# Two blocks on one core: down products that end output by output, an adaptive row by dot products, one norm statistic in place of two roots, and a lead of two half blocks

## The chip, the cores and the metric

The kernel runs on one core of a Trainium2 chip. A core has five engines with a queue of their own each: TensorE (matrix products, page name PE, its weight loads PEld), VectorE (DVE), ScalarE (ACT), GpSimd (POOL) and SyncE (SP), which here issues DMAs. The engines meet only through semaphores. The metric is the device time of one execution in microseconds (us); lower is better.

## The reference

Two layers on a sequence of 512 tokens of width 1024. Each begins with an adaptive vector, from which shifts, scales and gates come. What the change touches is the feed-forward part of the first layer, the norm that closes it and the norm that opens the second layer:

```python
x = x + g2 * conv_glu(modulate(rms_norm(x, norm2_w), sh2, sc2), ffn_w_up, ffn_conv_w, ffn_conv_b, ffn_w_down)
return rms_norm(x, final_norm_w)              # end of the first layer
...
mod = (silu(c_2) @ ada_w_2 + ada_b_2)         # 6 x 1024 values for the second layer
sh1, sc1, g1, sh2, sc2, g2 = jnp.split(mod, 6, axis=-1)
h = rmsnorm(x, mix_norm_pre) * (1.0 + sc1) + sh1
x = x + g1 * rmsnorm(windowed_gqa_sink(h, w_qkv, ...), mix_norm_post)
h = rmsnorm(x, ffn_norm_pre) * (1.0 + sc2) + sh2
x = x + g2 * rmsnorm(swiglu(h, w_in, w_out), ffn_norm_post)
```

The hidden width is 2816, the weights are float32, and so is the result.

## The kernel before

Values lie transposed: channels on the 128 partitions, the 512 tokens along the row, so that a vector of 1024 channels is 8 chunks and the hidden layer 22.

**Products.** Weights come in 92 blocks of 1 MB (128 x 2048). A block in `w_raw` is copied to `w_hi` in a rounded format by ScalarE (`high`, L230), and POOL takes the rest, `w_lo = w_raw - w_hi`, in four instructions (`low`, L239). Activations are split likewise into `h_hi` and `h_lo`. A product is then three matrix products over a chunk, hi·hi, hi·lo and lo·hi (`chunk_products`, L246). Raw, hi and lo have two buffers each, used in turn: `high` and `low` of block b wait until block b-2 is used (`half_used`, counted twice a block), and SyncE loads block b when the split of block b-2 is done (`lo_done`).

**Stages.** Blocks 0 to 11 are the first projection (with context products, L1089, beside it), 12 to 15 the first output projection, 16 to 37 the first up product, 38 to 48 the first down product (L285), 49 to 54 the projection of the second layer, 55 to 58 its output projection, 59 to 80 and 81 to 91 the second up and down product. In the ordinary form a block gives two outputs of 128 channels over all 8 chunks, into banks 0 to 3 in turn. A stage that follows a norm opens with `lead`: as its input chunks come one by one (`h_low`), block b is done chunk by chunk for both outputs, then block b+1 output by output. In the down products a block holds two of the 22 hidden chunks for all 8 outputs; eight banks gather over 11 blocks, and the last block ends them 6 products apart. The hidden pair of each block goes through slots 0 to 3 of `h_hi` (ScalarE, L1375) and `h_lo` (VectorE, L1624).

**Norm.** ScalarE squares each output (L319), VectorE adds the squares (L332), TensorE makes the mean (`mean`, L338), ScalarE its root (L343), VectorE the reciprocal (L347), TensorE spreads it over a bank (`spread`, L354), VectorE scales (L376), ScalarE applies gain and shift in two versions (L363, L366), and VectorE subtracts them (L379). Between the layers two norms follow each other. They are folded: squares with and without the final weight (L1404) are summed apart, and four small steps give a common scale (`fold`).

**The second adaptive vector.** Its weights come as 24 tiles through a ring of two (`ada_ring`, L214). VectorE adds each tile in eight steps of 256 columns to `acc2` (`add_ada2`, L1459 and L1461), one tile after the tap sums of each gated tile of the first up product, and two after it. After the down product TensorE sums `acc2` over the partitions, 48 columns (L1227), and VectorE makes the gains (L1666 to L1671).

The order of the work is written by hand, one program for each engine; every queue is in order. SyncE's loads alternate: a weight block, an adaptive tile.

## Time and profile before

| | us |
|---|---|
| runs shown | 1529.8, 1535.93, 1533.78 (median 1533.78) |
| the profiled execution | 1530.2, of which span 1528.4 |
| busy: PE / DVE / ACT / POOL | 1406.1 / 651.7 / 555.5 / 634.2 |
| granted TensorE clock, mean share | 0.948 |

The durations further on come from the profiled execution. PE is busy for 92% of its span; a busy PE is not PE at its peak, since matrix products are pipelined and their ends are modelled. An instruction for TensorE on float32 data stands as two records in the trace, on the rounded format as one.

### The profile page before, as it was taken

To read this page: it belongs to the slowest core of one execution; us is meant where nothing else is said; L and a number is where in the kernel's file an instruction comes from. 1 tells how busy PE (TensorE), PEld (TensorE's weight loads), DVE (VectorE), ACT (ScalarE), POOL (GpSimd) and SP (SyncE) were. 2 spreads that over 40 slices of the span, in tenths; PEclk is the share of its full clock that TensorE was granted. 3 is DMA by queue.
4 is the path that set the end of the run, shared out by engine and by line. 5 is a ranking of instruction groups with operands and counts; after the bars stand their busy time and mean duration, and the time that the engine had idled before them with its cause. 6 is when DMAs were issued, how large, how long until landed. Compare 5 with 4: busy or idle time off the path is not lost.

```text
span 1528.4 us, 17743 instructions
## 1 busy us (share of the span) xinstructions
PE 1406.1 (92%) x6432; PEld 1130.5 (74%) x6432; DVE 651.7 (43%) x1173; ACT 555.5 (36%) x807; POOL 634.2 (41%) x516
## 2 busy tenths in 40 slices
PE   8699997898678899999899989999979999999995
PEld 1588866686677678888688888655768888888884
DVE  1563478576842665554711163476232000001115
ACT  2512423473322544344222262477235232323221
POOL 0233254124634254545445554433242444444642
PEclk9799998899989899999999979999969999999997
DMA  9124552600012145545422232200111232222221
GB/s 396 55 99 173 194 193 105 166 1 1 1 56 110 64 185 219 206 178 194 192 83 108 82 138 83 83 2 1 52 59 55 85 107 84 108 86 107 83 82 55
DMA packets 26979, 165.45 MB, mean 108 GB/s; under 512 B 2688, under 2 KB 4992, under 8 KB 8496
## 3 DMA queue, kind: packets, MB, share of 16 engines
q1 hardware_dynamic: 24912, 150.10, 26.7%
q10 hardware_dynamic: 2016, 14.68, 2.7%
q8 instruction: 31, 0.51, 0.1%
q14 instruction: 20, 0.16, 0.0%
HBM read 162.64 MB, written 6.32 MB: 111 GB/s over the span
## 4 chain that ended last, share of the span: by engine, by line
PE 82%; DVE 7%; POOL 4%; issue 3%; ACT 2%; DMA 1%; POOLq 0%; SPq 0%; DVEq 0%; ACTq 0%
PE bank L246 46%; PE bank L285 16%; PE bank L1089 3%; PE bank L583 2%; PE bank L563 2%; PE bank L1067 2%; PE bank L444 2%; POOL arena L761 1%; PE bank L1227 1%; POOL arena L763 1%; PE bank L1149 1%; PE bank L573 1%; PE bank L423 1%; PE bank L424 1%; PE bank L354 1%
## 5 line engine op out<-in xcount | busy, mean ns | idle before, releaser
L239 POOL TENSOR_TENSOR w_lo<-w_raw,w_hi 128x512 fp32r<-128x512 f32 x368 | 499.2, 1387 | 693.0 <-ACT w_hi L230 683.1
L246 PE MATMUL bank<-h_hi,w_hi 128*128 128x512 f32 x1120 | 443.9, 396 | 22.6 <-POOL w_lo L239 8.7
L246 PE MATMUL bank<-h_lo,w_hi 128*128 128x512 f32 x1120 | 439.5, 392 | 0.0
L246 PE MATMUL bank<-h_hi,w_lo 128*128 128x512 f32 x1120 | 439.4, 392 | 0.0
L230 ACT ACTIVATE w_hi<-w_raw 128x2048 fp32r<-128x2048 f32 x92 | 176.2, 1915 | 439.4 <-PE bank L285 172.1
L246 PEld LDWEIGHTS bank<-h_hi,w_hi 128*128 128x128 f32 x1120 | 212.8, 190 | 71.9 <-issue 17.2
L246 PEld LDWEIGHTS bank<-h_hi,w_lo 128*128 128x128 f32 x1120 | 212.3, 190 | 44.8
L246 PEld LDWEIGHTS bank<-h_lo,w_hi 128*128 128x128 f32 x1120 | 212.6, 190 | 43.3
L285 PE MATMUL bank<-h_hi,w_hi 128*128 128x512 f32 x352 | 138.0, 392 | 7.2 <-DVE arena L1635 6.3
L285 PE MATMUL bank<-h_lo,w_hi 128*128 128x512 f32 x352 | 137.7, 391 | 0.0
L285 PE MATMUL bank<-h_hi,w_lo 128*128 128x512 f32 x352 | 137.5, 391 | 0.0
L1624 DVE TENSOR_TENSOR h_lo<-arena,h_hi 128x1024 fp32r<-128x1024 f32 x22 | 31.5, 1438 | 183.1 <-ACT h_hi L1375 172.3
L1731 DVE TENSOR_TENSOR arena<-arena,bank 128x512 f32 (+1 forms) x22 | 15.2, 689 | 208.7 <-PE bank L246 208.7
L1461 DVE SCALAR_TENSOR_TENSOR arena<-ada_ring,small,arena 128x256 f32 (+1 forms) x168 | 92.4, 550 | 6.0
L285 PEld LDWEIGHTS bank<-h_hi,w_hi 128*128 128x128 f32 x352 | 66.5, 189 | 22.0 <-DVE arena L1635 6.7
L319 ACT ACTIVATE arena<-arena 128x512 f32<-128x512 f32 (+1 forms) x56 | 33.3, 598 | 122.9 <-DVE arena L1614 37.7
L285 PEld LDWEIGHTS bank<-h_hi,w_lo 128*128 128x128 f32 x352 | 66.5, 189 | 14.0
L285 PEld LDWEIGHTS bank<-h_lo,w_hi 128*128 128x128 f32 x352 | 66.5, 189 | 13.6
L1470 DVE SCALAR_TENSOR_TENSOR arena<-bank,params,arena 128x511 f32<-128x511 f32 (+1 forms) x36 | 25.4, 704 | 119.6 <-ACT arena L1352 87.0
L719 POOL TENSOR_SCALAR arena<-arena,small 128x256 f32<-128x256 f32 (+1 forms) x64 | 32.8, 531 | 55.4 <-DVE small L677 55.4
L539 POOL TENSOR_SCALAR arena<-arena,small 128x512 f32<-128x512 f32 x32 | 21.7, 692 | 73.3 <-DVE small L518 73.3
L1089 PE MATMUL bank<-arena,w_raw 128*128 128x256 f32 x224 | 50.5, 379 | 0.0
(222 smaller groups left out, 1661.5 us busy)
## 6 DMA issues: line engine op xcount, KB each, us to landing
w_raw<-w_dram SPq DMA_DIRECT2D x92, 1024.0 KB, 4.8
ada_ring<-ada_dram SPq DMA_DIRECT2D x30, 1024.0 KB, 4.8
ada_ring<-ada_dram ACTq DMA_DIRECT2D x14, 1024.0 KB, 4.7
arena<-ada_dram SPq DMA_DIRECT2D x4, 1024.0 KB, 9.4
arena<-x_dram SPq DMA_DIRECT2D x2, 2048.0 KB, 11.5
bias_copies<-bias_rows SPq DMA_DIRECT2D x1, 4096.0 KB, 26.3
arena<-bias_copies SPq DMA_DIRECT2D x1, 3072.0 KB, 11.3
out_dram<-arena SPq DMA_DIRECT2D x8, 256.0 KB, 2.1
```

The costliest lines, as they stand in the source:

```text
L230: nc.scalar.activation(w_hi[b % 2][:], w_raw[b % 2][:], ACT.Copy).then_inc(hi_done, 1)
L239: last = nc.gpsimd.tensor_tensor(w_lo[b % 2][:, part], w_raw[b % 2][:, part], w_hi[b % 2][:, part], ALU.subtract)
L246: last = nc.tensor.matmul(bank[:, :], w[:, ft, k, :], x[:, k, :], start=k == 0 and m == 0, stop=k == DC - 1 and m == 2)
L285: last = nc.tensor.matmul(ps[f][:, :], w[:, k, f, :], x[:, 2 * gslot + k, :], start=first and k == 0 and m == 0, stop=last_block and k == ...
L319: nc.scalar.activation(buf[:, k % 2, 0:n], src, ACT.Square).then_inc(sq_done, 1)
L444: last = nc.tensor.matmul(ps[7][:, 0:256], v, pt1[G % 2][:, kb, :], start=kb == 0, stop=kb == 3)
L563: nc.tensor.matmul(ps[u % 3][:, 0:128 * (hi - lo)], q2[:, 2 * g + hq // 2, t * 128:(t + 1) * 128], k2[:, g, hq % 2, lo * 128:hi * 128], st ...
L583: last = nc.tensor.matmul(ps[7][:, :], vtok2[:, lo + kb, g, :], pt2[:, G % 2, kb, :], start=kb == 0, stop=kb == hi - lo - 1)
L719: nc.gpsimd.tensor_scalar(prob2[:, u % 8, 0:w], prob2[:, u % 8, 0:w], row_inv[:, u % 16:u % 16 + 1], 1.0, ALU.mult, ALU.mult).then_inc(s[" ...
L1089: last = nc.tensor.matmul(ps[4 + n % 2][:, 0:CTX], raw[:, n % 2, k, :], HC[:, k, :], start=k == 0, stop=k == DC - 1)
L1461: ins = nc.vector.scalar_tensor_tensor(out=dst, in0=src, scalar=silu_c2[:, k:k + 1], in1=dst, op0=ALU.mult, op1=ALU.add)
L1624: nc.vector.tensor_tensor(h_lo[:, part, :], HID[:, bass.ds(2 * t + 2 * off, 2), :], h_hi[:, part, :], ALU.subtract).then_inc(g_split, 1)
```

## The change

- **Down products.** The hidden weights are laid out anew: 7 blocks by chunk pair as before (chunks 0 to 13), then 4 blocks in the ordinary form (chunks 14 to 21, all eight slots of `h_hi`). So the outputs end one after the other, 24 products apart, and the updates and squares of the first seven run under the products. The very first products go to banks 4 to 7; only those for banks 0 to 3 wait for the last gated tile.
- **The statistic.** The mean is made in two parts: `mean_head` over the sum of seven squares, in the stream before the last chunks, and `mean_last` directly from the eighth square. VectorE adds seven, not eight.
- **The folded norm.** The root for the next input is taken from one statistic: the squares of ScalarE are scaled by `sqrt(final^2 + eps)`, the epsilon is `eps^2`. The scale for the residual is a root of its own, taken after the third affine chunk, and its spread stands inside `lead`.
- **The adaptive vector.** Its weights are transposed, and each tile gives two groups of 128 values by two dot products with a row (`tensor_tensor_reduce`). The row `row2` is spread over all partitions by eight products in the first output projection and copied from two banks by ScalarE. Tiles 20 and 21 are moved behind the first two hidden splits of the down product, 22 and 23 behind its loop; both last loads stand behind both first down blocks.
- **The lead.** Now chunks 0 to 3 of block b, chunks 0 to 3 of block b+1, chunks 4 to 7 of b, then of b+1. This holds for all four leads.
- A dummy root (`sqrt_table`) stands ahead of the squares, so that the table is loaded there.

```diff
-        def lead(pe, b, h_from, ctx_product=None):
+        def lead(pe, b, h_from, ctx_product=None, between=None):
             pe.wait_ge(lo_done, b + 1)
-            for k in range(DC):
+            for k in range(4):
+                pe.wait_ge(h_low, h_from + k + 1)
+                for ft in (0, 1):
+                    chunk_products(b, ft, ps[ft], k)
+            if between:
+                between()
+            pe.wait_ge(lo_done, b + 2)
+            for k in range(4):
+                for ft in (0, 1):
+                    chunk_products(b + 1, ft, ps[2 + ft], k)
+            for k in range(4, DC):
                 if k == DC - 1 and ctx_product:
                     ctx_product(0)
                     ctx_product(1)
...
                     last = chunk_products(b, ft, ps[ft], k)
                     if k == DC - 1:
                         last.then_inc(half_used, 1)
-            pe.wait_ge(lo_done, b + 2)
             for ft in (0, 1):
                 if ctx_product:
                     ctx_product(2 + ft)
-                for k in range(DC):
+                for k in range(4, DC):
                     last = chunk_products(b + 1, ft, ps[2 + ft], k)
                 last.then_inc(half_used, 1)
...
+                return
+            for k in range(2):
+                for f in range(4, DC):
+                    product(k, f)
+            pe.wait_ge(tile_free, bank_free)
+            for k in range(2):
+                for f in range(4):
+                    last = product(k, f)
+                last.then_inc(half_used, 1)
...
+        def mean_head(pe, r, buf, bank):
+            pe.wait_ge(sq_used, 8 * r + 7)
+            for t in range(4):
+                nc.tensor.matmul(ps[bank][:, t:t + 1], buf[:, 2, t * P:(t + 1) * P], con_("mean")[:, 0:1], start=t == 0, stop=False)
+        def mean_last(pe, r, buf, bank):
+            pe.wait_ge(sq_done, 8 * r + 8)
+            for t in range(4):
+                last = nc.tensor.matmul(ps[bank][:, t:t + 1], buf[:, 1, t * P:(t + 1) * P], con_("mean")[:, 0:1], start=False, stop=t == 3)
+                if t == 2:
+                    last.then_inc(sq_used, 1)
+            last.then_inc(mean_done, 1)
...
                 load_block(sp, B_DOWN + u)
+            for u in range(2):
                 load_ada(sp, T["ada2"][22 + u], 46 + u)
             with sp.Fori(0, 5) as i:
                 for u in range(2):
                     load_block(sp, B_DOWN + 2 + u, 2 * i)
             load_block(sp, 50)
             sp.wait_ge(mod2_ready, 1)
+            sp.wait_ge(g_split, 11)
...
+                    down_products(pe, b0 + t, 0, t, bank_free if t == 0 else None)
...
                     for t in (2, 3):
-                        pe.wait_ge(g_split, g0 + t + 1 + 2 * i)
-                        down_products(pe, b0 + t, 2 * i, t % 2, False, False)
...
+                down_products(pe, b0 + 6, 0, 0)
+                pe.wait_ge(lo_done, b0 + 8)
+                for k in (4, 5, 6, 7, 2, 3, 0, 1):
+                    if k in (2, 0):
+                        pe.wait_ge(g_split, g0 + (10 if k == 2 else 11))
+                    for ft in (0, 1):
+                        last = chunk_products(b0 + 7, ft, ps[ft], k, None, 1)
+                        if k == 1:
+                            last.then_inc(half_used, 1)
+                for f in range(2, DC):
+                    b = b0 + 7 + f // 2
+                    if f % 2 == 0:
+                        pe.wait_ge(lo_done, b + 1)
+                    for k in range(DC):
+                        last = chunk_products(b, f % 2, ps[f], k, None, DC - 1)
+                        if f == DC - 1 and k == 5:
+                            mean_head(pe, r, SQ2, 4)
+                    last.then_inc(half_used, 1)
+                mean_last(pe, r, SQ2, 4)
...
+            for k in range(DC):
+                last = nc.tensor.matmul(ps[5 + k // 4][:, k % 4 * P:(k % 4 + 1) * P], silu_c2[:, k:k + 1].to_broadcast([P, P]), ident,
+                                        start=True, stop=True)
+            last.then_inc(row2_done, 1)
...
-            pe.wait_ge(down_free, 1)
-            pe.wait_ge(ada_used, 48)
-            for f in range(48):
-                last = nc.tensor.matmul(ps[0][:, f:f + 1], acc2[:, f * 128:(f + 1) * 128], ones[:, 0:1], start=True, stop=True)
-            last.then_inc(col_done, 1)
...
+            down(B_DOWN, 0, 3, F_QKV)
+            spread(pe, 3, 5).then_inc(scale_out, 1)
...
+                last = nc.tensor.matmul(ps[4][:, 4 + t:5 + t], SQF[:, 2, t * P:(t + 1) * P], con_("mean")[:, 0:1], start=True, stop=True)
+            last.then_inc(res_mean, 1)
+            def residual_spread():
+                pe.wait_ge(res_scale, 1)
+                spread(pe, 3, 6, of=res_col).then_inc(scale_out, 1)
+            lead(pe, B_QKV, 16, between=residual_spread)
...
+            nc.scalar.activation(final_eps, par_("final"), ACT.Square).then_inc(root_final, 1)
+            act.wait_ge(root_final, 1)
+            nc.scalar.activation(final_eps, final_eps, ACT.Sqrt, bias=con_("eps")).then_inc(root_final, 1)
...
+                act.wait_ge(half_used, 2 * b0)
+                hidden_high(slice(18, 20), 4)
+                hidden_high(slice(20, 22), 6)
                 high(act, b0 + 2)
...
+                        act.wait_ge(half_used, 2 * b0 + 2 * (t - 1) + 4 * i)
+                        hidden_high(bass.ds(2 * t + 4 * i, 2), 2 * (t % 2))
                         high(act, b0 + t + 1, 2 * i)
...
+                sqrt_table()
+                high(act, b0 + 8)
+                high(act, b0 + 9)
+                for f in range(3):
+                    squares_of(f)
+                high(act, b0 + 10)
+                squares_of(3)
+                squares_of(4)
+                if blocks_after:
+                    high(act, b0 + 11)
+                for f in range(5, DC):
+                    squares_of(f)
+            sqrt_table()
+            for k in range(2):
+                act.wait_ge(row2_done, 1)
+                nc.scalar.activation(row2[:, 512 * k:512 * k + 512], ps[5 + k][:, :], ACT.Copy).then_inc(row2_out, 1)
...
+            def both_squares(f):
                 act.wait_ge(down_free, f + 1)
-                squares(act, 3, f, XR[:, f, :], SQ2)
+                squares(act, 3, f, XR[:, f, :], SQ2, scale=final_eps[:, f:f + 1])
...
-                nc.scalar.activation(SQF[:, f % 2, :], XR[:, f, :], ACT.Square, scale=par_("final")[:, f:f + 1]).then_inc(sqf_done, 1)
...
+                nc.scalar.activation(SQF[:, f % 2, :], XR[:, f, :], ACT.Square).then_inc(sqf_done, 1)
...
+            down_act(B_DOWN, F_QKV, both_squares, True)
+            root(act, 3, 4, eps="epseps")
+            high(act, B_QKV + 1)
...
+            def residual_root():
+                act.wait_ge(res_mean, 1)
+                nc.scalar.activation(res_col, ps[4][:, 4:8], ACT.Sqrt, bias=con_("eps")).then_inc(res_root, 1)
+            affine(act, 2, lambda c: gain3[:, c:c + 1], lambda c: mod2[:, c:c + 1], XN2, HB2, residual_root)
...
-                dst = acc2[:, bass.ds(256 * j + 256 * off, 256)]
-                for k in range(8):
...
-                    ins = nc.vector.scalar_tensor_tensor(out=dst, in0=src, scalar=silu_c2[:, k:k + 1], in1=dst,
-                                                         op0=ALU.mult, op1=ALU.add)
...
+                for f in range(2):
+                    src = ada[:, s * BLK + f * D:s * BLK + (f + 1) * D]
+                    last = nc.vector.tensor_tensor_reduce(out=src, in0=src, in1=row2, scale=1.0, scalar=0.0, op0=ALU.mult,
+                                                          op1=ALU.add, accum_out=dots[:, 2 * s + f:2 * s + f + 1])
+                last.then_inc(ada_used, 1)
+                dve.wait_ge(ada_used, 24 + j + 1 + off)
+                two = bass.ds(2 * j + 2 * off, 2)
+                nc.vector.tensor_tensor(mod2[:, two], dots[:, 2 * s:2 * s + 2], par_("adab2")[:, two], ALU.add).then_inc(mod2_part, 1)
...
-                add_ada2(u, 2 * i)
+                if u < 2:
+                    add_ada2(u, 2 * i)
...
+                hidden_low(g0 + 3, slice(18, 20), 4)
+                hidden_low(g0 + 4, slice(20, 22), 6)
+                if with_ada:
+                    add_ada2(20)
+                    add_ada2(21)
...
                 if with_ada:
                     add_ada2(22)
                     add_ada2(23)
...
+                    dve.wait_ge(mod2_part, 24)
...
+                hidden_low(g0 + 9, slice(12, 14), 0)
+                hidden_low(g0 + 10, slice(16, 18), 2)
+                hidden_low(g0 + 11, slice(14, 16), 0)
...
+                dve.wait_ge(half_used, 2 * (B_DOWN + 7) + f + 1)
...
+            normalise(dve, 2, XR, XN2, HB2, 5, residual_scale)
```

The queue of SyncE around the first two down blocks. `ada_ring<-ada_dram` is a load of an adaptive tile, `w_raw<-w_dram` one of a weight block. Before:

```order
L214 ISA
L214 DMA ada_ring<-ada_dram 128x2048
L990 REGISTER_ALU
L990 COMPARE_AND_BRANCH
L223 DMA w_raw<-w_dram 128x2048
L214 DMA ada_ring<-ada_dram 128x2048
L223 DMA w_raw<-w_dram 128x2048
L214 DMA ada_ring<-ada_dram 128x2048
L997 UNCONDITIONAL_BRANCH
L997 ISA
L223 ISA
L223 DMA w_raw<-w_dram 128x2048
```

And now:

```order
L214 ISA
L214 DMA ada_ring<-ada_dram 128x2048
L1018 REGISTER_ALU
L1018 COMPARE_AND_BRANCH
L223 DMA w_raw<-w_dram 128x2048 x2
L214 DMA ada_ring<-ada_dram 128x2048 x2
L1026 UNCONDITIONAL_BRANCH
L1026 ISA
L223 ISA
L223 DMA w_raw<-w_dram 128x2048
L223 ISA
L223 DMA w_raw<-w_dram 128x2048
```

Two weight loads (blocks 38 and 39) stand together, and two adaptive loads behind them, ahead of the loop that begins with block 40.

TensorE at the end of the first down product: L285 is a down product, L1227 the column sums, L1232 and L338 the two statistics, L354 the spreads, L246 the projection. Before:

```order
L285 MATMUL bank<-h_hi,w_lo 128x512
L285 MATMUL bank<-h_hi,w_hi 128x512
L285 MATMUL bank<-h_lo,w_hi 128x512
L285 MATMUL bank<-h_hi,w_lo 128x512
L1227 MATMUL bank<-constants,arena 128x1 x48
L1232 MATMUL bank<-constants,ada_ring 128x1 x4
L338 MATMUL bank<-constants,arena 128x1 x4
L354 MATMUL bank<-constants,small 128x128 x8
L246 MATMUL bank<-h_hi,w_hi 128x512
```

And now (L350 is `mean_head`, L356 `mean_last`, L378 the spread, L1294 the other statistic):

```order
L246 MATMUL bank<-h_lo,w_hi 128x512
L246 MATMUL bank<-h_hi,w_lo 128x512
L350 MATMUL bank<-constants,arena 128x1 x4
L246 MATMUL bank<-h_hi,w_hi 128x512
L246 MATMUL bank<-h_lo,w_hi 128x512
L246 MATMUL bank<-h_hi,w_lo 128x512
L246 MATMUL bank<-h_hi,w_hi 128x512
L246 MATMUL bank<-h_lo,w_hi 128x512
L246 MATMUL bank<-h_hi,w_lo 128x512
L356 MATMUL bank<-constants,arena 128x1 x4
L378 MATMUL bank<-constants,small 128x128 x4
L1294 MATMUL bank<-constants,ada_ring 128x1 x4
L246 MATMUL bank<-h_hi,w_hi 128x512
```

The column sums and one spread are gone from here, and half a statistic stands six products before the end.

ScalarE at the first output projection (L863 and L891 split its input, L319 and L324 are squares, L230 the weight copy). Before:

```order
L863 ACTIVATE h_hi<-arena 128x512 x4
L319 ACTIVATE arena<-arena 128x512 x2
L230 ACTIVATE w_hi<-w_raw 128x2048
L319 ACTIVATE arena<-arena 128x512 x2
L230 ACTIVATE w_hi<-w_raw 128x2048
```

And now (L362 the dummy root, L1473 the copies of `row2`):

```order
L891 ACTIVATE h_hi<-arena 128x512 x4
L362 ACTIVATE small<-constants 128x1
L1473 ACTIVATE arena<-bank 128x512 x2
L324 ACTIVATE arena<-arena 128x512 x2
L230 ACTIVATE w_hi<-w_raw 128x2048
L324 ACTIVATE arena<-arena 128x512 x2
L230 ACTIVATE w_hi<-w_raw 128x2048
```

The root and the two copies stand ahead of the first square.

## Rows read from the trace of the kernel before

**Rows 1.** Chain in order of time, whole span: start us, us, what.
```profile
74.39 3.45 PE bank L1089 x16
...
474.00 24.01 PE bank L246 x96
...
757.99 121.62 PE bank L285 x528
879.61 15.79 PE bank L1227 x96
...
906.57 66.05 PE bank L246 x288
...
1388.98 119.99 PE bank L285 x528
```

**Rows 2.** TensorE's waits: waiting line <- releaser: us, times, longest.
```profile
PE bank L246 <- POOL w_lo L239: 8.7, 4, 5.2
...
PE bank L285 <- DVE arena L1635: 6.3, 1, 6.3
...
PE bank L285 <- DVE arena L1731: 0.9, 1, 0.9
```

**Rows 3.** Chain, 500 to 510 us.
```profile
499.48 0.70 DVE arena L332
...
500.22 1.07 PE bank L338 x8
...
507.03 3.33 PE bank L246 x7
```

**Rows 4.** Timelines of ScalarE and POOL, 905 to 1180 us.
```profile
918.29 1.92 ACT L230 ACTIVATE w_hi<-w_raw 128x2048 fp32r<-128x2048 f32 x1 [2.53 <-PE bank L246]
...
1120.28 1.28 ACT L343 ACT_TABLE_LOAD   x1
...
1158.97 0.60 ACT L1357 ACTIVATE arena<-bank 128x512 f32<-128x512 f32 x1 [1.98 <-PE bank L246]
...
1161.65 5.03 POOL L239 TENSOR_TENSOR w_lo<-w_raw,w_hi 128x512 fp32r<-128x512 f32 x4 [26.07 <-ACT w_hi L230]
```

**Rows 5.** Timelines near 37, 463, 901 us: spreads and first square.
```profile
37.14 1.16 PE L354 MATMUL bank<-constants,small 128*128 128x128 f32 x8
...
463.60 0.63 ACT L319 ACTIVATE arena<-arena 128x512 f32<-128x512 f32 x1 [12.26 <-DVE arena L1614]
...
901.29 3.76 PE L354 MATMUL bank<-constants,small 128*128 128x128 f32 x16 [2.27 <-DVE small L1680]
```

**Rows 6.** Timeline, 515 to 535 us: start, us, work [idle before].
```profile
520.22 1.28 ACT L1352 ACT_TABLE_LOAD   x1 [4.01 <-PE bank L246]
...
532.28 0.50 PE L246 MATMUL bank<-h_hi,w_hi 128*128 128x512 f32 x1 [0.71 <-POOL w_lo L239]
```

**Rows 7.** Chain, 518 to 560 us.
```profile
527.02 1.41 DVE arena L1461
...
530.54 6.74 DMA w_raw<-w_dram
```

**Rows 8.** Page, DMA issues: count, KB each, us to landing.
```profile
w_raw<-w_dram SPq DMA_DIRECT2D x92, 1024.0 KB, 4.8
```

**Rows 9.** VectorE by form, 976 to 1070 us: ...count | busy us, mean ns.
```profile
L663 DVE CUSTOM_DVE_ANT_0 bank<-bank,arena,small 128x384 f32<-128x384 f32 x32 | 19.7, 616 | 2.6 <-PE bank L563 1.9
L663 DVE CUSTOM_DVE_ANT_0 bank<-bank,arena,small 128x256 f32<-128x256 f32 x32 | 15.5, 483 | 2.0 <-PE bank L563 1.7
...
L663 DVE DVE_READ_ACCUMULATOR2_ANT small<- 128x1 f32 x64 | 8.2, 129 | 0.3
```

**Rows 10.** Timeline of POOL, 725 to 800 us.
```profile
754.29 5.46 POOL L239 TENSOR_TENSOR w_lo<-w_raw,w_hi 128x512 fp32r<-128x512 f32 x4 [6.28 <-ACT w_hi L230]
773.01 6.02 POOL L239 TENSOR_TENSOR w_lo<-w_raw,w_hi 128x512 fp32r<-128x512 f32 x4 [13.26 <-ACT w_hi L230]
```

**Rows 11.** Chain, 749 to 760 us.
```profile
747.37 2.86 DVE h_lo L1624 x2
```

More of the change, by code:

```diff
@@ L56 @@
 CCOL, _at = {}, 0
-for _n, _w in [("ident", 128), ("trif", 128), ("trib", 128), ("ones", 128), ("mean", 128), ("mean512", 128), ("eps", 1)]:
+for _n, _w in [("ident", 128), ("trif", 128), ("trib", 128), ("ones", 128), ("mean", 128), ("mean512", 128), ("eps", 1), ("epseps", 1)]:
     CCOL[_n] = (_at, _w)
@@ L240, in low, with chunk_products @@
             last.then_inc(lo_done, 1)
-        def chunk_products(b, ft, bank, k):
+        def chunk_products(b, ft, bank, k, first=0, final=DC - 1):
             hi, lo = (w[b % 2][:, :].rearrange("p (f k n) -> p f k n", f=2, k=DC) for w in (w_hi, w_lo))
             for m, (w, x) in enumerate(((hi, h_hi), (hi, h_lo), (lo, h_hi))):
-                last = nc.tensor.matmul(bank[:, :], w[:, ft, k, :], x[:, k, :], start=k == 0 and m == 0, stop=k == DC - 1 and m == 2)
+                last = nc.tensor.matmul(bank[:, :], w[:, ft, k, :], x[:, k, :], start=k == first and m == 0, stop=k == final and m == 2)
             return last
@@ L284, in product @@
                 for m, (w, x) in enumerate(((hi, h_hi), (hi, h_lo), (lo, h_hi))):
-                    last = nc.tensor.matmul(ps[f][:, :], w[:, k, f, :], x[:, 2 * gslot + k, :], start=first and k == 0 and m == 0,
-                                            stop=last_block and k == 1 and m == 2)
-                return last
-            if last_block:
-                for f in range(DC):
-                    a, b = product(0, f), product(1, f)
-                    if f < DC - 1:
-                        b.then_inc(down_done, 1)
-                    else:
-                        a.then_inc(half_used, 1)
-                        b.then_inc(half_used, 1)
-            else:
+                    last = nc.tensor.matmul(ps[f][:, :], w[:, k, f, :], x[:, 2 * gslot + k, :],
+                                            start=bank_free is not None and k == 0 and m == 0, stop=False)
+                return last
+            if bank_free is None:
                 for k in range(2):
@@ L355, in spread, with affine @@
             return last
-        def affine(act, m, gain, shift, xn, hb):
+        def affine(act, m, gain, shift, xn, hb, aside=None):
             for c in range(DC):
@@ L1034, in _, with plain_sum @@
             ssd_pool()
-            lows(B_OUT + 2, 36)
-            for f in range(DC):
+            lows(B_OUT + 2, 32)
+            def plain_sum(f):
                 pool.wait_ge(sqf_done, f + 1)
@@ L1265, in _ @@
             last_turn(B_UP2 + 20, F_UP2 + 40)
-            pe.wait_ge(tile_free, F_UP2 + 44)
-            down(B_DOWN2, 11)
-            mean(pe, 6, SQ2, 4)
+            down(B_DOWN2, 11, 6, F_UP2 + 44)
             spread(pe, 6, 4).then_inc(scale_out, 1)
@@ L1393, in _ @@
             glu(B_UP, F_UP, True, 1)
-            down_act(B_DOWN, F_QKV)
-            high(act, 49)
-            high(act, 50)
-            for f in range(DC):
+            def both_squares(f):
                 act.wait_ge(down_free, f + 1)
-                squares(act, 3, f, XR[:, f, :], SQ2)
+                squares(act, 3, f, XR[:, f, :], SQ2, scale=final_eps[:, f:f + 1])
                 if f == 0:
@@ L1737, in _ @@
             gated2(20)
[L1738 to L1739 removed]
+            hidden_low(12, slice(0, 2), 0)
+            hidden_low(13, slice(2, 4), 2)
             gated2(21)
```

184 lines of the change are left out of this document (90 added, 94 removed).

## The prediction

> **What bounds the kernel.** I read the page first, then TensorE's waits, then the chain in order of time, and only then timelines of the places that the change touches. In TensorE's long loops nothing waits: 528 products in 119.99 us, 0.227 us each [rows 1]. The time outside them lies at the seams, so the change is worth what it does at the seams. Four concern us: the second tiles of each product stage, which wait for the split of the weights (8.7 us in four waits), the start of the first down product (6.3 us), that of the second (0.9 us) [rows 2], and the passage from the first down product to the next projection, where the chain goes through 96 column sums and a norm and the next products start at 906.57 [rows 1].
>
> **1. The passage after the first down product.** The 96 column sums begin at 879.61 and the projection at 906.57: 26.96 us [rows 1]. The sums go (the row is made by dot products on VectorE, which is idle there), the second root of the folded norm goes, and the outputs end 5.4 us apart, so that only the last one's square is left. What is late next is the plain norm path, which the trace shows once: the output projection ends at 498.01 (474.00 and 24.01) [rows 1] and its norm lets the next products start at 507.03 [rows 3], 9.02 us; less the addition of the last square (0.70 and its hand-over, 0.74) [rows 3], which becomes an accumulating product: 8.28. Gain **18.7**. ScalarE's next weight copy (1.92) [rows 4] lies between its root and the first affine, in the time of the spread. The sum of plain squares on POOL, its memset and the second spread's statistic end before TensorE has finished the first spread, by some 1 us.
>
> **2. That projection's lead.** The residual's spread (one, 8 records) now stands inside it: 1.2 us by the fast row, 1.9 by the slow one [rows 5]; 1.2. The products begin after only short work and pauses, as at 507.03, where seven took 3.33 us [rows 3], 0.43 to 0.48 each, TensorE at its lower clock level. The two down stages give the price of such a start: 121.62 against 119.99, 1.6 [rows 1]; cost **2.8** in all (0.6 if the clock stays up, as at the old seam).
>
> **3. The new lead order.** Weights have two buffers. Block b's buffer is free for block b+2 only when b is used up. Before, b was used up 10.9 us before the lead ended (48 products of 0.227); now its last four chunks come after half of b+1, and 5.44 us are left. Copy and split take longer, 1.92 + 5.03 and two hand-overs, 7.15 us from 918.29 on [rows 4], so the projection's third block waits 1.75. In the second up product it is 7.7 us from the SiLU at 1158.97 to the end of the split at 1166.68 [rows 4], against 6.1 (5.44 and the other tile's 3 products): **1.7**. In the first up product two table loads and the taps stand ahead of the copy: 520.22 to 532.28 [rows 6], 12.3 us with what lies between the tile's end and the load, against 11.6 before (a stall of 0.7 [rows 6]) and 6.1 now. That stall grows by 5.4, long enough for the lower clock at its end (1.6); the next block's wait, part of the 8.7 [rows 2], was for a load queued behind an adaptive one [rows 7], and goes (1.3): **+5.7**. In the first projection two context tiles (3.45 each [rows 1]) and 24 products, 12.3 us, and a small product of 1 us stand behind the used-up block, against a load (4.8 [rows 8]), a copy, a split and hand-overs, 12.5: 0. Sum **9.2**.
>
> **4. The output projection.** Eight transposing products (16 records) stand between the two blocks of its lead, 2.3 us by the fast row, 3.8 by the slow one [rows 5]. TensorE waits there anyway (one of the four waits for a split). But ScalarE waits for them, then copies two banks (0.6 each), and only then takes the first square, which was at 463.60 [rows 5]. Squares, VectorE's updates, the weight copy and POOL's split follow one another, so the third block, which started after a wait for that split, moves by all of it: TensorE ends the first block at 463.4, plus 2.3 and 1.1 is 466.8: **+3.2** (+4.7 by the slow row).
>
> **5. Start of the down products.** They begin with banks 4 to 7 (24 products, 5.4 us), under which the last gated tile, freed of its adaptive step, is ready. Gain 6.3 and the slow start 1.6 [rows 1, 2], and 0.9 at the second: **-8.8**. VectorE's 168 small multiply-adds become 48 dot products; none bounds the up product, so that is worth nothing there. A dot of 1024 is sized by the same form at 384 and 256 columns, 616 and 483 ns: 1.04 ns a column on 217 ns gives 1.28 us, and 0.13 for the accumulator's read [rows 9]; a tile of two is 3.0 us with its sum.
>
> **6. What is queued behind those dots.** SyncE's queue is in order. The loads of adaptive tiles 22 and 23 now both stand ahead of weight block 40, and wait for the dots of tiles 20 and 21, which VectorE now does after two more splits of the hidden values. ScalarE is free for their copies when POOL starts its split, 754.3 [rows 10]; a copy of 1.04 and two splits of 1.43 [rows 11] end at 758.0. The first dot meets the rest of POOL's split, and there an instruction with two sources took 1.41 for 256 columns [rows 7]; I take 2.4 for it, 1.28 for the other three, 0.5 for four reads and 0.6 for two sums and their waits: 765.4. The load of block 40 goes out at 766, and lands 6.7 us after its issue when an adaptive load is beside it [rows 7]: 772.7. Copy 1.92 and split 6.02 [rows 4, 10] with hand-overs give 781.0. TensorE, started at 751.55, wants it two blocks later, at 773.3: a stall of 7.7 and a slow start, **+9.3**. Bounds: dots untouched and a landing in 4.8 us [rows 8], 4.5; dots twice as long, 13.5.
>
> **7. Small ones.** A statistic over seven outputs stands in the stream of each down product: 2 x 1.05 (eight records of such a mean take 1.07 [rows 3]) = **+2.1**. The last norm of all saves its addition, **-0.7**; in the output projections ScalarE's weight copy ends after the statistic, so nothing. The root's table load at 1120.28 [rows 4] goes from the path: **-1.3**.
>
> **Sum** in the profiled execution: -18.7 + 2.8 + 9.2 + 3.2 - 8.8 + 9.3 + 2.1 - 0.7 - 1.3 = **-2.9**, so 1530.2 becomes 1527.3 (span 1525.5). The median of the runs is 1533.78, 3.6 above that execution: I predict **1530.9**.
>
> **A rule against the change.** The dots sized above have one source in PSUM; the new ones have both in SBUF. The Trainium skill (Vector Engine (DVE) Microarchitecture Reference, "Points that are easy to get wrong") says that the scalar-tensor-tensor form with two non-bf16 SBUF sources runs at half rate, as no read port is left for the accumulator. No row here has this form; by it each dot would be nearer 2.4 us.
>
> **Rivals.** (A) The load behind the dots is hardly late. For it: the old queue order gave block 40 a slack of 2.7 us after a late start, and a dot away from POOL takes 1.28. Then step 6 is 4.5, and with the clock staying up in step 2, the total is -2.9 - 4.8 - 2.2 = -9.9: **1523.9**. Against it: the two adaptive loads need the whole of both tiles first.
> (B) It ends slower: dots of two SBUF sources take twice as long. Step 6 becomes 13.5 (+4.2), and in the first up product the load behind the first tile's dots arrives late again, which gives back the 1.3 and 0.5 more (+1.8): -2.9 + 6.0 = +3.1, **1536.9**. The 6.0 is linear between 1.28 and 2.4 us a dot, so the sign turns at 1.82. For it: instructions of two SBUF sources stretched to 1.41 beside POOL [rows 7]; against it: the split of 1024 hidden columns, both sources in SBUF, takes 1.43 [rows 11], no half rate, though it does not accumulate. This is what the skill's rule would do here.
> (C) The lead order costs nothing, because high and low copies find time: total -2.9 - 9.2 = -12.1, **1521.7**. Against it stand the two-buffer waits, which no other work can shorten; I see no way round them.
>
> **Chances.** Forecast 0.60, A 0.17, B 0.12, C 0.06, something not seen 0.05. Less than 0.5% (7.7 us) can't be told from no change in this kernel. The forecast's own range is 1525 to 1537; A and C are mostly beyond 0.5% on the fast side; B is within it, unless the slow rows or a further wait join. Faster 0.25, within 0.63, slower 0.12. The range goes from C's total to beyond B's, with the slow rows of steps 2 and 4 on top of it: 1520 to 1541.
>
> **What would show it.** Right: no column sums in the chain and the projection starting some 8.5 us after the down product; a wait of some 7 us of the third down block for POOL's split, with SyncE's load of that block issued near 15 us after the down start; waits for the split of 6, 1.7 and 1.7 us at the ends of three leads; a longer wait in the output projection; dots of 1.3 us. Wrong: dots of 2.4 us (B), a third down block without wait (A), leads without waits (C), or a norm path longer than 9 us after the first down product, where I take the trace's other norm as the measure. If the passage gains less than 15 us, the total is no gain at all.

## The result, and the profile after

The changed kernel takes 1536.4 us (median of 20 runs), the kernel before 1531.97 in the same number of runs: ratio 1.0023, 95% interval 1.0015 to 1.0031. I had forecast 1530.9, 3 us less than before; it is some 4 us more. The profiled execution has a span of 1533.7 us (before 1528.4). In some executions the first attention takes 4 to 7 us longer at a lower granted clock (0.59 to 0.64 from 264 to 300 us, against 0.74 to 0.77 in the others), and the profiled ones of three experiments (old leads, row2 late, new lead alone) are of that kind, so I compare stages, not whole spans.

TensorE's waits of the changed kernel (waiting line <- releaser: us in total, times, longest), which answer to [rows 2]:

```profile
PE bank L246 <- POOL w_lo L239: 18.6, 5, 7.6
...
PE bank L294 <- POOL w_lo L239: 9.9, 1, 9.9
PE bank L246 <- DVE h_lo L405: 9.8, 3, 4.2
```

The down products (now L294) no longer wait for the gated tile, as before at their start, but once for a split, for longer. The waits of the ordinary products for a split went from 8.7 to 18.6 us.

Its chain in order of time (start us, us, what), against [rows 1, 3]:

```profile
478.33 24.51 PE bank L246 x96
...
544.22 214.40 PE bank L246 x936
...
795.86 57.08 PE bank L294 x240
...
898.99 1.07 PE bank L356 x8
900.61 2.09 PE bank L378 x8
905.05 1.53 DVE h_lo L405
906.72 7.37 PE bank L246 x24
...
933.13 45.47 PE bank L246 x192
...
1177.37 217.92 PE bank L246 x960
```

No column sums stand between the last down product (it ends at 897.39) and the projection at 906.72; in their place other pieces begin behind waits: at 544.22, 795.86, 933.13 and 1177.37. Set against the same products of before, stage by stage (from the starts and ends of the products in the two traces; the forecast is the sum of its terms there):

| stage | before | after | change | forecast |
|---|---|---|---|---|
| first projection, to its last split | 171.53 | 172.44 | +0.91 | 0 |
| to the first output projection | 220.15 | 220.80 | +0.65 | 0 |
| its first two blocks, to the third | 27.77 | 30.51 | +2.74 | +3.2 |
| its rest and the norm | 33.03 | 33.54 | +0.51 | 0 |
| first up product | 244.65 | 252.01 | +7.36 | +5.7 |
| wait before the down products | 6.31 | 0 | -6.31 | -6.3 |
| first down product | 121.62 | 133.51 | +11.89 | +8.75 |
| passage to the projection | 26.96 | 9.33 | -17.63 | -18.7 |
| that projection | 69.50 | 75.33 | +5.83 | +4.55 |
| second attention | 97.17 | 97.18 | +0.01 | 0 |
| second output projection, norms | 73.27 | 72.39 | -0.88 | -1.3 |
| second up product | 241.59 | 243.67 | +2.08 | +1.7 |
| second down product, with its start | 120.85 | 120.62 | -0.23 | +0.15 |
| the rest (and 0.03 of the start) | | | -1.63 | -0.7 |
| sum | | | +5.3 | -2.95 |

Every stage for which the forecast had over a microsecond moved its way. But every cost except one came out larger (the first down product by 3.1 us, the first up product by 1.7, the projection by 1.3), and the largest gain smaller by 1.1. The 0.91 of the first projection lies in its first products, 66 of them in 17.93 us, where another execution with the same order (row2 late) needs 16.77, neither with a wait in between: TensorE stayed at the lower clock level for longer.

### The profile page after: what moved, and what is told of

Read it like the earlier page. It is cut to its first block, busy times and chain, and to the rows that moved or that the text cites. A ratio compares the mean times of both kernels' runs of the same rounds, so it can differ in the third digit from the quotient of the medians.

```text
span 1533.7 us, 17381 instructions
## 1 busy us (share of the span) xinstructions
PE 1402.9 (91%) x6384; PEld 1126.1 (73%) x6384; DVE 621.7 (41%) x1093; ACT 557.4 (36%) x815; POOL 636.8 (42%) x516
## 4 chain that ended last, share of the span: by engine, by line
PE 81%; POOL 5%; DVE 5%; issue 4%; ACT 3%; DMA 2%; POOLq 0%; ACTq 0%; SPq 0%; DVEq 0%
PE bank L246 53%; PE bank L294 9%; PE bank L1133 3%; PE bank L611 2%; POOL w_lo L239 2%; PE bank L591 2%; PE bank L472 2%; POOL arena L789 1%; PE bank L1111 1%; ACT w_hi L230 1%; DMA ada_ring<-ada_dram 1%; PE bank L1193 1%; POOL arena L791 1%; PE bank L601 1%; PE bank L1320 1%
## 5 line engine op out<-in xcount | busy, mean ns | idle before, releaser
L246 PE MATMUL bank<-h_hi,w_hi 128*128 128x512 f32 x1248 | 496.7, 398 | 34.3 <-POOL w_lo L239 18.6
L246 PE MATMUL bank<-h_lo,w_hi 128*128 128x512 f32 x1248 | 491.7, 394 | 0.0
L246 PE MATMUL bank<-h_hi,w_lo 128*128 128x512 f32 x1248 | 491.3, 394 | 0.0
L230 ACT ACTIVATE w_hi<-w_raw 128x2048 fp32r<-128x2048 f32 x92 | 176.1, 1914 | 394.7 <-PE bank L246 198.0
L246 PEld LDWEIGHTS bank<-h_hi,w_hi 128*128 128x128 f32 x1248 | 238.5, 191 | 88.2 <-issue 19.6
L246 PEld LDWEIGHTS bank<-h_hi,w_lo 128*128 128x128 f32 x1248 | 237.9, 191 | 50.4
L246 PEld LDWEIGHTS bank<-h_lo,w_hi 128*128 128x128 f32 x1248 | 238.4, 191 | 49.3
L294 PE MATMUL bank<-h_hi,w_hi 128*128 128x512 f32 x224 | 88.3, 394 | 9.9 <-POOL w_lo L239 9.9
L294 PE MATMUL bank<-h_lo,w_hi 128*128 128x512 f32 x224 | 88.1, 393 | 0.0
L294 PE MATMUL bank<-h_hi,w_lo 128*128 128x512 f32 x224 | 88.0, 393 | 0.0
L324 ACT ACTIVATE arena<-arena 128x512 f32<-128x512 f32 (+1 forms) x48 | 28.2, 593 | 116.2 <-DVE arena L1806 34.1
L1553 DVE CUSTOM_DVE_ANT_0 ada_ring<-ada_ring,arena 128x1024 f32<-128x1024 f32 x48 | 62.1, 1330 | 0.0
L294 PEld LDWEIGHTS bank<-h_hi,w_hi 128*128 128x128 f32 x224 | 42.7, 191 | 19.5 <-POOL w_lo L239 10.3
L294 PEld LDWEIGHTS bank<-h_hi,w_lo 128*128 128x128 f32 x224 | 42.6, 190 | 8.9
L294 PEld LDWEIGHTS bank<-h_lo,w_hi 128*128 128x128 f32 x224 | 42.6, 190 | 8.9
## 6 DMA issues: line engine op xcount, KB each, us to landing
arena<-bias_copies SPq DMA_DIRECT2D x1, 3072.0 KB, 13.5
```

Source lines behind the costliest of these rows:

```text
L230: nc.scalar.activation(w_hi[b % 2][:], w_raw[b % 2][:], ACT.Copy).then_inc(hi_done, 1)
L246: last = nc.tensor.matmul(bank[:, :], w[:, ft, k, :], x[:, k, :], start=k == first and m == 0, stop=k == final and m == 2)
L294: last = nc.tensor.matmul(ps[f][:, :], w[:, k, f, :], x[:, 2 * gslot + k, :], start=bank_free is not None and k == 0 and m == 0, stop=False)
L324: nc.scalar.activation(buf[:, k % 2, 0:n], src, ACT.Square, scale=scale).then_inc(sq_done, 1)
L1553: last = nc.vector.tensor_tensor_reduce(out=src, in0=src, in1=row2, scale=1.0, scalar=0.0, op0=ALU.mult, op1=ALU.add, accum_out=dots[:, 2 ...
```

## The experiments

All were timed in the same rounds as the kernel before (1531.6 us median in the first four, 1531.92 in the last four). "The changed kernel" is the 1536.4 us above; it was timed apart from them, beside a kernel before of 1531.97.

**The old leads.**

```diff
-            for k in range(4):
-                pe.wait_ge(h_low, h_from + k + 1)
-                for ft in (0, 1):
-                    chunk_products(b, ft, ps[ft], k)
-            if between:
-                between()
-            pe.wait_ge(lo_done, b + 2)
-            for k in range(4):
-                for ft in (0, 1):
-                    chunk_products(b + 1, ft, ps[2 + ft], k)
-            for k in range(4, DC):
+            for k in range(DC):
...
+                if k == 3 and between:
+                    between()
+            pe.wait_ge(lo_done, b + 2)
             for ft in (0, 1):
...
-                for k in range(4, DC):
+                for k in range(DC):
```

> The changed kernel with the lead in the order of the kernel before, in all four stages that open with one; the residual's spread stays behind chunk 3 of the first block. Theory 1 (the new order uses up the first block's buffer 5.4 us too late, and the third block waits for its copy and split): the third block's waits of 0.96, 1.79 and 1.65 us in the first, second-layer and second up projection go, that of the first up product falls from 7.56 to about 2.1 us (its copy and split now take 13.5 us from the first tile's end, against 12.1 before), and the slow-clock starts behind two of them (1.6 each) go: 12 to 14 us less than the changed kernel's 1536.4, about 1523.5. Theory 2 (the waits come mainly from the split beside the dot products, which stays): the first up product keeps some 5 us and its slow start, total 6 us less, about 1530.

Measured: 1522.88 us, ratio to before 0.9931 (0.9914 to 0.9947), so 13.5 less than the changed kernel. The wait of the first up product's third block is 2.21 us, where theory 1 gave about 2.1 (timeline: start, us, work, [idle before]):

```profile
541.26 0.50 PE L246 MATMUL bank<-h_hi,w_hi 128*128 128x512 f32 x1 [2.21 <-POOL w_lo L239]
```

By stage against the changed kernel: first up product -7.0, the projection -3.65, the second up product -1.8, together 12.5. Of the 7.0, 5.35 are the wait; 1.4 is a faster start of the stage behind its norm, which isn't the order's doing, as the three edits together (below) have the old leads and the slow start there. The slow start behind the wait of 2.21 us stayed, against theory 1. In stages that the edit doesn't touch this execution is 1.3 faster in the first projection, 1.7 in the down product and 1.2 in the passage, and 4.9 slower from the first attention to the norm behind it; the traces show the clock in the first and the last, and for the down product a wait of 9.06 in place of 9.92. Theory 2 is out: the order costs it. One number in my text was misread, though: the 0.96 us in the first projection is no wait but a small product that the kernel before has too, so that stage has nothing to give.

**The new lead alone, in the kernel before.** The same edit the other way.

> The kernel before with one part of the change alone, the new order of the lead. Theory 1 (the order costs by itself, through two buffers): the third block waits about 1, 6.2, 1.8 and 1.7 us in the four stages, with a slow-clock start behind at least the longest; the wait of 1.18 us further on in the first up product goes: 10 to 13 us more than the kernel before, about 1543.5. Theory 2 (the order costs little without the dot products and the residual's spread of the full change): under 6 us more, below 1538.

Measured: 1540.75 us, ratio 1.0047 (1.0032 to 1.0061); the medians differ by 9.15, the interval allows 4.9 to 9.3. By the stages that hold the edit it is +9.9: +6.9 in the first up product, +1.8 in the projection, +1.6 in the second up product, -0.4 in the first projection. That is a little less than theory 1's lower end and far from theory 2: the projection's wait had no slow start behind it here, and the first projection has no wait. Its longest wait, with the old accumulation on VectorE:

```profile
546.93 0.79 PE L246 MATMUL bank<-h_hi,w_hi 128*128 128x512 f32 x1 [6.05 <-POOL w_lo L239]
```

**Block 40's load ahead.**

```diff
                 load_block(sp, B_DOWN + u)
+            load_block(sp, B_DOWN + 2)
             for u in range(2):
                 load_ada(sp, T["ada2"][22 + u], 46 + u)
+            load_block(sp, B_DOWN + 3)
...
```

> The changed kernel with one change in the queue of SyncE: the load of weight block 40 stands ahead of the loads of adaptive tiles 22 and 23, block 41 behind them. Theory 1 (the third down block waits 9.9 us because its load is queued behind loads that wait for dot products): block 40's load goes out when block 38 is split, some 3 us before the down products begin, the wait falls to under 0.5 us and the slow-clock start (1.6) goes: 11 to 12.5 us less, about 1524.5. Theory 2 (the copy of block 40 is late on ScalarE and its split on POOL, which takes 8 us beside VectorE, whatever the load does): a wait of 3 to 6 us stays, 4 to 7 us less, about 1531.

Measured: 1522.97 us, ratio 0.9935 (0.992 to 0.9949), 13.4 less. Changed kernel, chain from 767 us on:

```profile
767.49 3.79 DVE h_lo L1716 x2
771.28 2.23 DVE ada_ring L1553
773.52 2.22 DVE ada_ring L1553
...
775.94 1.14 DVE ada_ring L1553
777.09 1.14 DVE ada_ring L1553
...
779.37 7.43 DMA w_raw<-w_dram
...
786.83 1.92 ACT w_hi L230
...
790.13 1.42 POOL w_lo L239
...
792.34 3.48 POOL w_lo L239 x2
...
795.86 4.21 PE bank L294 x9
```

Read it downwards: hidden splits, four dots, the load (it was free to go when block 38 was split, before 761), its landing, copy, split, TensorE. With the load ahead, the timeline of that kernel shows the copy 11.6 us earlier, waiting for its buffer and no longer for a load, the split right behind it, and no wait of TensorE in the down product:

```profile
775.22 1.92 ACT L230 ACTIVATE w_hi<-w_raw 128x2048 fp32r<-128x2048 f32 x1 [6.61 <-PE bank L294]
...
777.30 7.06 POOL L239 TENSOR_TENSOR w_lo<-w_raw,w_hi 128x512 fp32r<-128x512 f32 x4 [2.44 <-ACT w_hi L230]
```

The stage is 12.5 us shorter, as theory 1 had it. The other 1.2 came in the passage, of which more below.

**Short dots.**

```diff
-                    src = ada[:, s * BLK + f * D:s * BLK + (f + 1) * D]
+                    src = ada[:, s * BLK + f * D:s * BLK + f * D + 8]
-                    last = nc.vector.tensor_tensor_reduce(out=src, in0=src, in1=row2, scale=1.0, scalar=0.0, op0=ALU.mult,
+                    last = nc.vector.tensor_tensor_reduce(out=src, in0=src, in1=row2[:, 0:8], scale=1.0, scalar=0.0, op0=ALU.mult,
```

> The changed kernel with dot products over 8 columns in place of 1024; most of the second adaptive vector's sum is left out, nothing else. Theory 1 (the dots are what the queue waits for: 7.1 us between the hidden splits and the loads, two of them stretched to 2.2 us beside POOL, and they stretch POOL's split too): the third down block's wait falls from 9.9 to about 2.6 us, the third block's wait in the first up product from 7.6 to 6.1; 9 to 10.5 us less, about 1527. Theory 2 (the position of the two loads and their landing time of 7 us make the delay, the dots little): a wait above 7 us stays, under 4 us less, about 1533.

Measured: 1533.06 us, ratio 1.0005 (0.9995 to 1.0014), 3.3 less than the changed kernel. That is theory 2, which had named 1533. The third down block still waits:

```profile
791.54 0.79 PE L294 MATMUL bank<-h_hi,w_hi 128*128 128x512 f32 x1 [6.79 <-POOL w_lo L239]
```

Its chain says why: the load goes out 5.4 us earlier, but takes 8.51 to land with both adaptive loads on the way (7.43 with the long dots), and TensorE is itself 1.2 us earlier (the shorter wait in the up product):

```profile
770.22 1.17 DVE ada_ring L1553
...
773.97 8.51 DMA w_raw<-w_dram
```

So of the 9.92 us only 3.1 go with the long dots; 6.8 stay as long as the load stands behind the two others, and go when it is moved (above). In the first up product the wait fell from 7.56 to 5.62, though the stage is only 1.0 shorter, as the products behind the wait start 0.9 slower. There POOL's split, from 537.2 on, is what changed; first the changed kernel, then this one:

```profile
537.27 6.89 POOL L239 TENSOR_TENSOR w_lo<-w_raw,w_hi 128x512 fp32r<-128x512 f32 x4 [26.10 <-ACT w_hi L230]
```

```profile
537.20 4.95 POOL L239 TENSOR_TENSOR w_lo<-w_raw,w_hi 128x512 fp32r<-128x512 f32 x4 [26.09 <-ACT w_hi L230]
```

**row2 late.**

```diff
-            for k in range(DC):
-                last = nc.tensor.matmul(ps[5 + k // 4][:, k % 4 * P:(k % 4 + 1) * P], silu_c2[:, k:k + 1].to_broadcast([P, P]), ident,
...
             for ft in (0, 1):
                 for k in range(4, DC):
                     last = chunk_products(B_OUT + 1, ft, ps[2 + ft], k)
                 last.then_inc(half_used, 1)
+            for k in range(DC):
+                last = nc.tensor.matmul(ps[5 + k // 4][:, k % 4 * P:(k % 4 + 1) * P], silu_c2[:, k:k + 1].to_broadcast([P, P]), ident,
...
-            for k in range(2):
-                act.wait_ge(row2_done, 1)
...
                 if n % 2:
                     high(act, B_OUT + n // 2 + 2)
+                if n == 3:
+                    for k in range(2):
+                        act.wait_ge(row2_done, 1)
...
```

> The changed kernel with the eight products that spread row2 moved behind the second block of the first output projection, into the time in which TensorE waits for the third block's split, and ScalarE's two copies moved behind the weight copy of block 15. Theory 1 (the products and copies stand on the way of squares, updates, weight copy and split): the third block starts 2.7 us earlier, total 2.5 to 3 us less, about 1533.7. Theory 2 (only the 2.0 us of TensorE count, and they count wherever they stand; the wait is set by the squares alone): the wait grows by what the products save, 0 to 0.7 us less, about 1536.

Measured: 1533.06 us, ratio 1.0009 (0.9992 to 1.0025), 3.3 less. The wait went down although TensorE now comes to it with the products done; the first row is the changed kernel, the second this one:

```profile
478.33 0.77 PE L246 MATMUL bank<-h_hi,w_hi 128*128 128x512 f32 x1 [5.91 <-POOL w_lo L239]
```

```profile
480.03 0.47 PE L246 MATMUL bank<-h_hi,w_hi 128*128 128x512 f32 x1 [3.39 <-POOL w_lo L239]
```

The products themselves now lie in the waiting time. The stage is 2.5 shorter up to the third block and 0.9 behind it, where the slow start is less. Theory 1.

**Column sums back.**

```diff
+                if r == 3:
+                    pe.wait_ge(down_free, 1)
+                    for f in range(48):
+                        nc.tensor.matmul(ps[0][:, f:f + 1], ident, con_("mean")[:, 0:1], start=True, stop=True)
                 mean_last(pe, r, SQ2, 4)
```

> The changed kernel with 48 one-column float32 products (96 records, as the removed column sums, here on constants and unused) put back between the last down product and the last square's part of the statistic. Theory 1 (the sums lay wholly on the path, 15.79 us, and what is saved in the passage is mainly these): they now cover the 1.6 us in which TensorE waits for the last square, so 14 us more, about 1550.5. Theory 2 (the passage is bound by the norm's hand-overs, and the sums would lie beside them): 7 us more or less, below 1544.

Measured: 1553.58 us, ratio 1.0131 (1.0117 to 1.0146), 17.2 more, 16.9 of it between the down product's last wait and the projection: theory 1, and above its 14. The sums took longer than the 15.79 of [rows 1], as the granted clock fell to 0.50 within their first 4 us, and the eight records behind them took 1.85 instead of 1.07 at that level:

```profile
896.27 17.79 PE L1266 MATMUL bank<-constants 128*128 128x1 f32 x96
913.92 1.85 PE L356 MATMUL bank<-constants,arena 128*128 128x1 f32 x8
```

**The three edits together.** Old leads, block 40's load ahead, row2 late.

> The changed kernel with the three edits of the first experiments together: the old order of the leads, block 40's load ahead of the two adaptive loads, row2's products and copies moved behind. Theory 1 (the three costs lie at different seams and add up): 1522.9 + 1523.0 + 1533.1 - 2 x 1536.4 = 1506.2 us, the first up product's third block waiting some 2.2 us and the third down block none. Theory 2 (they hide one another: what one gives back, the next wait takes): above 1512.

Measured: 1507.48 us, ratio 0.9834 (0.982 to 0.9848). Within 1.4 us of the sum of the single ones: the costs lie at different seams.

**And two weight copies moved.**

```diff
+                if n == 0:
+                    high(act, B_OUT + 2)
                 act.wait_ge(tile_free, F_OUT + n + 1)
                 squares(act, 2, n, XR[:, n, :], SQ2)
-                if n % 2:
+                if n in (3, 5):
                     high(act, B_OUT + n // 2 + 2)
...
             root(act, 2, 4)
+            high(act, B_OUT + 5)
```

> The version of the three edits with two more moves on ScalarE in the first output projection: the weight copy of block 14 ahead of the first square, not behind the second, and the copy of block 17 behind the norm's root. Theory 1 (the third block waits for squares, then copy, then split; the root waits 0.6 us for a copy): the wait before block 14 falls from 3.4 by some 1.5 to 2 us and the norm by 0.6: 2 to 2.6 us less than the three edits alone, about 1504. Theory 2 (the copy waits for the same end of the two blocks as the squares, and what the squares lose comes back in the updates): no change, about 1506.

Measured: 1499.03 us, ratio 0.979 (0.9773 to 0.9807): 2.1% faster than the kernel before (1.9 to 2.3), and by the medians 8.5 us faster than the three edits, where 2 to 2.6 were expected. With five runs each, which spread over 4.5 and 6.2 us, that difference is rough: the fastest runs differ by 7.0, the profiled spans by 11.3. The wait before block 14, 3.40 us with the three edits, is now

```profile
471.65 0.47 PE L246 MATMUL bank<-h_hi,w_hi 128*128 128x512 f32 x1 [0.73 <-POOL w_lo L239]
```

2.7 less, and the norm behind is 1.0 shorter: 3.7 us by the mechanism of theory 1. What was not: after the short wait the clock stays up. Stretches of 4 us behind that wait (us, busy of PE, PEld, DVE, ACT, POOL, then PEclk), first with the three edits, then here:

```profile
475.90:479.90 4.00, 3.95 (x11) 3.20 (x12) 0.00 (x0) 0.00 (x0) 4.00 (x4) 0.62 0.69 240
```

```profile
471.60:475.60 4.00, 3.95 (x18) 3.30 (x18) 2.04 (x3) 2.58 (x4) 0.00 (x0) 1.00 0.69 244
```

11 products against 18, which makes the block's stage 1.7 shorter. The other 5.9 us between the two profiled executions lie where nothing was edited: 1.4 up to the first output projection, 1.7 in the passage, 1.2 in the projection, 0.7 and 0.6 in the two up products and small rests; such pieces vary between executions (below), and no run tells how much of them belongs to the edit.

## Why the prediction was wrong

By its steps:

- **1, the passage: right.** -17.63 against -18.7, and the column sums on the path are confirmed by putting them back. The rest was sized at 8.28 and took 9.33: the granted clock was already 0.50 from 900 to 903 us, when the spread ran, 2.09 us. In the kernel with block 40's load ahead, where the passage took 8.11, it was still 0.89 there:

```profile
888.25 1.16 PE L378 MATMUL bank<-constants,small 128*128 128x128 f32 x8 [0.57 <-DVE small L370]
```

- **2, the residual's spread and the slow start: right.** 96 products and the spread took 24.62, 2.8 above the pace.
- **3, the new leads: failed in two terms.** Forecast 9.2; taking the order back gave 12.5 in the stages. The chain (buffer used up late, then copy, then split) was right: the waits of 1.80 and 1.66 us are the forecast 1.75 and 1.7, and in the first up product the order alone adds 5.34 (0.71 to 6.05, in the kernel before) or 5.35 (2.21 to 7.56, in the changed one), the forecast 5.4. Missing was, first, what the dots do to POOL, put at nothing: with the old leads the wait is 2.21 us, in the kernel before it was 0.71, and POOL's split in front of it takes 6.98 us in place of 5.48; 1.5 us. With short dots it takes 4.95. Second, a slow start behind the 1.80 us wait of the projection, put at nothing: 1.6. The first projection has no wait, as forecast.
- **4, row2 in the output projection: right.** +2.74 at the third block, and 3.3 back when moved.
- **5, the start of the down products: right**, -6.31, and no wait at the second.
- **6, the load behind the dots: right in kind, the step that was undersized most.** Forecast 9.3 with the slow start; the stage says 12.4 (11.89 without the statistic and the old slow start), and undoing it gives 12.5 there. The wait was 9.92, not 7.7. Term by term: the load went out 15.5 us after the down products' start, not 14.45, for the two hidden splits took 1.56 and 2.31 beside POOL, where 1.43 each was taken (from the last hidden split to the load, four dots and their sums, 8.1 us passed, and 8.0 were forecast, though two of the dots took 2.3); it landed in 7.43, not 6.7; copy and split took 9.05, not 8.3; TensorE wanted it at 22.06, not 21.75. The start behind it, 9 products in 4.21 us, cost 2.2, not 1.6.
- **7:** the small ones came within half a microsecond each, except the end: -1.6, not -0.7. That end takes 17.8 to 19.1 us in the changed kernel's variants, where its code is the same, so the 0.9 can't be put down to the change.

The sign was wrong because gains and costs of some 30 us were set against each other for a net of -2.9, and each cost was taken at the length that its pieces had beside quiet neighbours. Steps 3 and 6 missed by 6.4 us between them, in the same direction and mostly for the same two reasons: VectorE and POOL slow each other, and behind three of the four new waits the products start slowly. That is more than the net. The stages for which nothing was forecast added another 2 (the first projection, the first attention, the norm), with no wait that is new there.

The total also looks nearer than it was. The forecast of -2.9 was put on a median of three runs, 1533.78; the twenty give 1531.97, and from there it would have been 1529.1, 7.3 below what was measured and not 5.5.

Of the rivals, A and C are out: the load was late, and the leads cost what they cost. B named the total (1536.9) by luck, not by its cause. The dots, all 48 (min, median and max in ns):

```profile
L1553 DVE CUSTOM_DVE_ANT_0 ada_ring<-ada_ring,arena x48: 1212/1219/2312, 534.5 to 831.5; 128x1024 f32<-128x1024 f32 x48
```

The median is 1.22 us for 1024 columns from two SBUF sources, below my 1.28. 43 of the 48 took 1.21 to 1.22; the other five, all beside POOL's split, 2.27 to 2.31. The Trainium skill's rule (Vector Engine (DVE) Microarchitecture Reference, "Points that are easy to get wrong") is on the scalar-tensor-tensor form with two SBUF sources that aren't bf16, and gives it half rate. The dots are of another form and show no half rate either. And I was wrong that no row had the rule's form: the old accumulation is one, L1461, with both sources in SBUF. In the kernel before (min, median and max in ns):

```profile
L1461 DVE SCALAR_TENSOR_TENSOR arena<-ada_ring,small,arena x168: 483/485/1452, 524.4 to 766.6; 128x256 f32 x140, 128x256 f32<-128x256 f32 x28
```

485 ns for 256 columns is what a form with one source in PSUM took, 483 [rows 9]. So this trace doesn't agree with the rule; the long ones, from 1366 ns on, lie beside POOL's split as the long dots do.

## What to carry to other kernels

Two buffers give the third block exactly the time that the second one still needs once the first is used up; any reordering that uses the first up later is paid for there, and so is a load that is queued behind one that waits. Add up copy, split and landing at the length they have beside their busy neighbours, and allow for a slow start of 1.6 to 2.9 us behind a new wait, though it doesn't come behind every one (last section). When a large gain comes out at nothing, list the seams of both traces side by side: here three of them held 29 us, each was undone by a few lines, and the sum of the three held within 1.4 us.

## What was not expected of the hardware

- An instruction of VectorE and one of POOL, both with two sources in SBUF, stretch each other. A dot takes 1.22 us or 2.3, the subtraction of 1024 hidden columns 1.21 with POOL quiet and up to 2.31, POOL's split 4.95 or 6.89. Even a dot of 8 columns, 0.16 us, takes 1.25 beside POOL's split, so the stretch doesn't go by the instruction's own length.
- What the clock does behind a wait isn't settled by its length alone. Mean granted clock in the 4 us behind a wait of 7.56, 1.80 and 1.66 us in the changed kernel:

```profile
544.20:548.20 4.00, 3.98 (x9) 3.14 (x10) 0.58 (x1) 1.91 (x1) 1.69 (x2) 0.50 1.01 354
933.10:937.10 4.00, 3.97 (x11) 3.16 (x12) 0.00 (x0) 0.24 (x1) 3.60 (x3) 0.63 0.69 246
1177.40:1181.40 4.00, 4.00 (x18) 3.29 (x19) 0.00 (x0) 1.54 (x2) 3.58 (x3) 1.00 0.62 242
```

9, 11 and 18 products in the same time: two waits that differ by 0.14 us, one with the lower level behind it and one without. The wait of 1.79 us in the kernel before with the new lead has full clock behind it (1.00, 17 products). And before the third block of the first up product, a wait of 2.21 us with the old leads and one of 2.23 with the three edits:

```profile
541.20:545.20 4.00, 3.94 (x12) 3.06 (x13) 0.62 (x2) 1.91 (x1) 1.80 (x3) 0.66 1.01 354
```

```profile
535.60:539.60 4.00, 3.98 (x17) 3.30 (x18) 0.58 (x1) 1.92 (x1) 1.77 (x2) 1.00 0.95 356
```

  What decides it stays open.
- The same passage, with equal instructions, took 8.1 us in three kernels, 9.3 in the changed one and two others, and 9.9 in one; the clock fell earlier in the long ones (the spread took 1.16 us in the short ones, 2.08 in the others). What sets that moment stays open.
